# Where weight slots and activations lie in SBUF, in a two-block transformer kernel on one core

## The reference, cut to what matters

```python
def first_block(x, ...):                      # 272 tokens
    a = rmsnorm(h, norm1[i])
    proj = a @ w_in[i]                        # pooling, two kinds of attention
    h = h + jnp.concatenate([y_pool, y_fox, y_sb], axis=-1) @ w_out[i]
    a = rmsnorm(h, norm2[i])
    h = h + (jax.nn.silu(a @ w_gate[i]) * (a @ w_up[i])) @ w_down[i]
...
def second_block(x, ...):                     # 256 tokens
    h = swiglu(rmsnorm_2(x, norm_ffn1_pre[l]), w_ffn1_in[l], w_ffn1_out[l])
    x = x + FFN_RESIDUAL_SCALE * rmsnorm_2(h, norm_ffn1_post[l])
    h = mixer(rmsnorm_2(x, norm_mix_pre[l]), w_mix_in[l], ...)
    x = x + rmsnorm_2(h, norm_mix_post[l])
    h = swiglu(rmsnorm_2(x, norm_ffn2_pre[l]), w_ffn2_in[l], w_ffn2_out[l])
```

## Time and profile before

| | us |
|---|---|
| median of 3 runs | 800.4 |
| lowest, highest | 800.27, 800.4 |
| span of the profiled execution | 798.0 |

### The profile page before, as it was taken

How to read it: one execution, slowest core, us unless ns; L and a number is a source line. 1 busy time by engine, 2 the same in 40 slices (tenths; PEclk the granted TensorE clock), 3 DMA queues, 4 the chain that set the end, 5 groups by cost and what they waited for, 6 DMA issues and landing times.

```text
span 798.0 us, 12187 instructions
## 1 busy us (share of the span) xinstructions
PE 787.6 (99%) x4716; PEld 693.5 (87%) x4716; DVE 531.7 (67%) x621; ACT 429.6 (54%) x565; POOL 29.7 (4%) x35
## 2 busy tenths in 40 slices
PE   8999999999999999999999999999999999999997
PEld 8989989888888888888888887999988888888885
DVE  7865557766666567866666566766977766666665
ACT  6556658454544548753544536565557644454444
POOL 0000100000000000000000000002420000000000
PEclk9999999999999999999999999999999999999999
DMA  8633333655545543665545554452444655554521
GB/s 332 238 118 126 123 115 138 224 186 183 209 167 203 187 181 113 237 234 181 209 165 204 187 181 159 148 195 106 159 178 152 225 210 177 191 197 172 209 105 53
DMA packets 20798, 141.16 MB, mean 177 GB/s; under 512 B 2449, under 2 KB 2705, under 8 KB 4385
## 3 DMA queue, kind: packets, MB, share of 16 engines
q1 hardware_dynamic: 20192, 138.65, 48.3%
q0 software_dynamic: 576, 2.10, 0.8%
HBM read 139.69 MB, written 1.05 MB: 176 GB/s over the span
## 4 chain that ended last, share of the span: by engine, by line
PE 95%; DVE 2%; ACT 2%; issue 1%; DMA 1%; SPq 0%; DVEq 0%; ACTq 0%
PE ps L1457 93%; ACT whi L679 1%; PE ps L1463 1%; DMA raw<-wstream 1%; DVE x L1206 0%; ACT squared L694 0%; DVE xa L1018 0%; PE ps L1694 0%; DVE wlo L1007 0%; PE ps L1664 0%; PE ps L1896 0%; DVE xg L1201 0%; DVEq L270 0%; ACT L912 0%; PE ps L1696 0%
## 5 line engine op out<-in xcount | busy, mean ns | idle before, releaser
L1457 PE MATMUL ps<-xa,whi 128*128 128x512 f32 (+2 forms) x1744 | 488.8, 348 | 0.0
L1457 PE MATMUL ps<-xa,wlo 128*128 128x256 f32 (+1 forms) x1376 | 383.1, 282 | 0.0
L1007 DVE TENSOR_TENSOR wlo<-raw,whi 128x2048 fp32r<-128x2048 f32 x128 | 293.1, 2290 | 83.8 <-ACT whi L679 83.6
L1457 PEld LDWEIGHTS ps<-xa,whi 128*128 128x128 f32 x1744 | 302.5, 188 | 44.6 <-issue 2.1
L1457 PEld LDWEIGHTS ps<-xa,wlo 128*128 128x128 f32 x1376 | 258.7, 189 | 1.1
L679 ACT ACTIVATE whi<-raw 128x2048 fp32r<-128x2048 f32 x128 | 244.2, 1908 | 7.0 <-PE ps L1457 6.8
L1457 PE MATMUL ps<-whi,hhi 128*128 128x512 f32 x240 | 93.8, 391 | 0.0
L1457 PE MATMUL ps<-whi,hlo 128*128 128x512 f32 x240 | 93.7, 390 | 0.0
L1457 PE MATMUL ps<-wlo,hhi 128*128 128x512 f32 x240 | 93.5, 390 | 0.0
L873 ACT ACTIVATE hhi<-arena 128x512 fp32r<-128x512 f32 x30 | 19.0, 633 | 89.0 <-PE ps L1457 82.5
L859 ACT ACTIVATE arena<-ps 128x512 f32<-128x512 f32 x33 | 19.7, 596 | 87.5 <-PE ps L1457 87.3
(11 more groups left out here) (216 smaller groups left out, 531.3 us busy)
## 6 DMA issues: line engine op xcount, KB each, us to landing
raw<-wstream SPq DMA_DIRECT2D x128, 1024.0 KB, 4.8
gain_row<-rows_in POOLq DMA_DIRECT2D x4, 512.0 KB, 3.8
x<-x_in SPq DMA_DIRECT2D x2, 512.0 KB, 4.0
raw<-wstream SPq DMA_DIRECT2D x2, 512.0 KB, 5.5
out<-x SPq DMA_DIRECT2D x4, 256.0 KB, 2.1
xg<-const_in SPq DMA_DIRECT2D x1, 912.0 KB, 11.7
small<-small_in SPq DMA_DIRECT2D x1, 152.0 KB, 6.0
arena<-meta_in SPq DMA_DIRECT2D x1, 64.0 KB, 4.6
```

Source lines behind the costliest of these rows:

```text
L1007: nc.vector.tensor_tensor(wlo[slot][:], raw[slot][:], whi[slot][:].bitcast(F32), ALU.subtract).then_inc(lo_ready, 1)
L1457: return nc.tensor.matmul(o, lhsT, rhs, start=start, stop=stop, skip_group_check=True)
```

## The change

Three edits, all of them on addresses.

1. `hhi` and `hlo` are made ahead of the slots. The slots are made in pairs `whi0, wlo0, whi1, wlo1, whi2, wlo2`, with a gap of 40 numbers (160 bytes) ahead of `whi1` and ahead of `whi2`. What is made later lies 320 bytes further on than it would without the gaps.
2. `xn[k]`, for norm k, is a view into the same memory as `xa`, with blocks 512 columns (2048 bytes) apart instead of 544, that starts at column 92, 104, 0 or 120 of it (368, 416, 0 and 480 bytes). `norm` and `hi_of` write `xn[k]`.
3. All that reads the activations behind the first stage reads `xn[k]`: the gate and up tiles with k = 0, 1 and 3, the mixer's units with k = 2. The first block's projection keeps `xa` with its blocks 544 columns apart.

The instructions of each engine, their shapes, their order and their semaphores are the same as before.

```diff
+SLOT_GAPS = (0, 40, 40)
+XN_AT = (92, 104, 0, 120)
...
-        whi = [sb(f"whi{s}", [P, UNIT], F32R) for s in range(SLOTS)]
-        wlo = [sb(f"wlo{s}", [P, UNIT], F32R) for s in range(SLOTS)]
+        hhi = sb("hhi", [P, 2, 256], F32R)
+        hlo = sb("hlo", [P, 2, 256], F32R)
+        whi, wlo = [], []
+        for s, gap in enumerate(SLOT_GAPS):
+            if gap:
+                sb(f"gap{s}", [P, gap])
+            whi.append(sb(f"whi{s}", [P, UNIT], F32R))
+            wlo.append(sb(f"wlo{s}", [P, UNIT], F32R))
         xa = sb("xa", [P, KT, 2 * TOK], F32R)
         ya = sb("ya", [P, KT, 2 * SEQ], F32R)
-        hhi = sb("hhi", [P, 2, 256], F32R)
-        hlo = sb("hlo", [P, 2, 256], F32R)
...
+        xa_line = xa[:].rearrange("p k c -> p (k c)")
+        xn = [xa_line[:, c:c + KT * 2 * SEQ].rearrange("p (k c) -> p k c", k=KT) for c in XN_AT]
...
-                    nc.scalar.activation(xa[:, kt, 0:SEQ], turn_place(k, kt), ACT.Copy, scale=vec(gain, kt)).then_inc(xa_hi_ready, 1)
+                    nc.scalar.activation(xn[k][:, kt, 0:SEQ], turn_place(k, kt), ACT.Copy, scale=vec(gain, kt)).then_inc(xa_hi_ready, 1)
...
-                        xa[:, kt, SEQ:2 * SEQ], turn_place(k, kt), vec(gain, kt),
-                        xa[:, kt, 0:SEQ].bitcast(F32), ALU.mult, ALU.subtract).then_inc(xa_ready, 1)
+                        xn[k][:, kt, SEQ:2 * SEQ], turn_place(k, kt), vec(gain, kt),
+                        xn[k][:, kt, 0:SEQ].bitcast(F32), ALU.mult, ALU.subtract).then_inc(xa_ready, 1)
...
-            def paired_tile(bank, slot, a):
+            def paired_tile(bank, slot, a, k):
...
-                    mm(ps[:, bank, :], whi[slot][:, w], xa[:, kt, 0:2 * SEQ], kt == 0, False)
-                    ins = mm(ps[:, bank, 0:SEQ], wlo[slot][:, w], xa[:, kt, 0:SEQ], False, kt == KT - 1)
+                    mm(ps[:, bank, :], whi[slot][:, w], xn[k][:, kt, 0:2 * SEQ], kt == 0, False)
+                    ins = mm(ps[:, bank, 0:SEQ], wlo[slot][:, w], xn[k][:, kt, 0:SEQ], False, kt == KT - 1)
...
-                    mm(o, xa[:, kt, hi], whi[slot][:, w], kt == 0, False)
-                    mm(o, xa[:, kt, hi], wlo[slot][:, w], False, False)
-                    ins = mm(o, xa[:, kt, lo], whi[slot][:, w], False, kt == KT - 1)
+                    mm(o, xn[2][:, kt, hi], whi[slot][:, w], kt == 0, False)
+                    mm(o, xn[2][:, kt, hi], wlo[slot][:, w], False, False)
+                    ins = mm(o, xn[2][:, kt, lo], whi[slot][:, w], False, kt == KT - 1)
```

More of the change, by code:

```diff
@@ L1480, in spread_rstd, with columns_tile @@
                 ins.then_inc(rstd_spread, 1)
-            def columns_tile(o, slot, a, n, skip=0):
+            def columns_tile(o, slot, a, of, n, skip=0):
                 for kt in range(KT):
                     w = slice(kt * 256 + a * P, kt * 256 + (a + 1) * P)
-                    mm(o, whi[slot][:, w], xa[:, kt, skip:n], kt == 0, False)
-                    mm(o, whi[slot][:, w], xa[:, kt, n + skip:2 * n], False, False)
-                    ins = mm(o, wlo[slot][:, w], xa[:, kt, skip:n], False, kt == KT - 1)
+                    mm(o, whi[slot][:, w], of[:, kt, skip:n], kt == 0, False)
+                    mm(o, whi[slot][:, w], of[:, kt, n + skip:2 * n], False, False)
+                    ins = mm(o, wlo[slot][:, w], of[:, kt, skip:n], False, kt == KT - 1)
                 return ins
-            def paired_tile(bank, slot, a):
+            def paired_tile(bank, slot, a, k):
                 for kt in range(KT):
                     w = slice(kt * 256 + a * P, kt * 256 + (a + 1) * P)
-                    mm(ps[:, bank, :], whi[slot][:, w], xa[:, kt, 0:2 * SEQ], kt == 0, False)
-                    ins = mm(ps[:, bank, 0:SEQ], wlo[slot][:, w], xa[:, kt, 0:SEQ], False, kt == KT - 1)
+                    mm(ps[:, bank, :], whi[slot][:, w], xn[k][:, kt, 0:2 * SEQ], kt == 0, False)
+                    ins = mm(ps[:, bank, 0:SEQ], wlo[slot][:, w], xn[k][:, kt, 0:SEQ], False, kt == KT - 1)
                 return ins
@@ L1507, in first_paired_unit @@
                         w = slice(kt * 256 + a * P, kt * 256 + (a + 1) * P)
-                        mm(ps[:, bank + a, 0:SEQ], whi[slot][:, w], xa[:, kt, 0:SEQ], kt == 0, False)
-                        mm(ps[:, bank + a, 0:SEQ], wlo[slot][:, w], xa[:, kt, 0:SEQ], False, False)
+                        mm(ps[:, bank + a, 0:SEQ], whi[slot][:, w], xn[k][:, kt, 0:SEQ], kt == 0, False)
+                        mm(ps[:, bank + a, 0:SEQ], wlo[slot][:, w], xn[k][:, kt, 0:SEQ], False, False)
                 for kt in range(KT):
@@ L1513, in first_paired_unit @@
                         w = slice(kt * 256 + a * P, kt * 256 + (a + 1) * P)
-                        ins = mm(ps[:, bank + a, SEQ:2 * SEQ], whi[slot][:, w], xa[:, kt, SEQ:2 * SEQ], False, kt == KT - 1)
+                        ins = mm(ps[:, bank + a, SEQ:2 * SEQ], whi[slot][:, w], xn[k][:, kt, SEQ:2 * SEQ], False, kt == KT - 1)
                 return ins
@@ L1528, in first_columns_unit @@
                         w = slice(kt * 256 + c, kt * 256 + c + P)
-                        mm(o, whi[slot][:, w], xa[:, kt, 0:SEQ], kt == 0 and c == 0, False)
-                        mm(o, wlo[slot][:, w], xa[:, kt, 0:SEQ], False, False)
+                        mm(o, whi[slot][:, w], xn[k][:, kt, 0:SEQ], kt == 0 and c == 0, False)
+                        mm(o, wlo[slot][:, w], xn[k][:, kt, 0:SEQ], False, False)
                 for kt in range(KT):
@@ L1534, in first_columns_unit @@
                         w = slice(kt * 256 + c, kt * 256 + c + P)
-                        ins = mm(o, whi[slot][:, w], xa[:, kt, SEQ:2 * SEQ], False, kt == KT - 1)
+                        ins = mm(o, whi[slot][:, w], xn[k][:, kt, SEQ:2 * SEQ], False, kt == KT - 1)
                 return ins
@@ L1642, in _ @@
                         skip = META if query else 0
-                        columns_tile(ps[:, i % 2, skip:TOK], n % SLOTS, i % 2, TOK,
+                        columns_tile(ps[:, i % 2, skip:TOK], n % SLOTS, i % 2, xa, TOK,
                                      skip).then_inc(unit_used if i % 2 else even_full, 1)
@@ L1777, in ffn @@
                 base, unit0 = f * GROUPS, U_FFN[f]
+                norm = (0, 1, 3)[f]
                 def two_tiles(unit, slot, bank, spread=False):
                     pe.wait_ge(lo_ready, unit + 1)
-                    paired_tile(bank, slot, 0)
+                    paired_tile(bank, slot, 0, norm)
                     if spread:
-                        spread_rstd((0, 1, 3)[f], 2)
-                    paired_tile(bank + 1, slot, 1).then_inc(unit_used, 1)
+                        spread_rstd(norm, 2)
+                    paired_tile(bank + 1, slot, 1, norm).then_inc(unit_used, 1)
                 def gate(g, unit, slot, first):
@@ L1803, in ffn @@
                 pe.wait_ge(lo_ready, unit0 + 1)
-                first_paired_unit(4, unit0 % SLOTS, (0, 1, 3)[f]).then_inc(unit_used, 1)
+                first_paired_unit(4, unit0 % SLOTS, norm).then_inc(unit_used, 1)
                 up(0, unit0 + 1, (unit0 + 1) % SLOTS)
@@ L1846, in _ @@
                                 ins.then_inc(mgate_done, 1)
-                            ins = columns_tile(ps[:, bank, a * SEQ:(a + 1) * SEQ], n % SLOTS, a, SEQ)
+                            ins = columns_tile(ps[:, bank, a * SEQ:(a + 1) * SEQ], n % SLOTS, a, xn[2], SEQ)
                     ins.then_inc(unit_used, 1)
@@ L1853, in _ @@
                         for part in range(2):
-                            ins = mm(ps[0:BACK + 16, 2, 0:SEQ], gate_w[:, kt, :], xa[:, kt, part * SEQ:(part + 1) * SEQ],
+                            ins = mm(ps[0:BACK + 16, 2, 0:SEQ], gate_w[:, kt, :], xn[2][:, kt, part * SEQ:(part + 1) * SEQ],
                                      kt == 0 and part == 0, kt == KT - 1 and part == 1)
```

## The result

The changed kernel takes 804.32 us (median of 4 runs, 804.27 to 804.64), beside 800.34 us of the kernel before: ratio 1.0053, 95% interval 1.0042 to 1.0065. It is slower by 4.0 us. 795.5 was forecast, with a range up to 804.

A forecast was written before the change was run, and what follows sets the result against it. The prediction took TensorE's own matmul steps to bound the kernel, with nothing upstream late. Its terms, -4.5 - 1.1 + 0 + 0.7 = -4.9 us, gave 798.0 - 4.9 + 2.4 = 795.5 us, range 788 to 804.

The forecast's parts named there:

- What bounds the kernel: Whole kernel: the time is the sum of TensorE's own matmul steps, busy 787.6 of 798.0 us, with nothing upstream late.
- The case in which nothing moves: Rival for the whole kernel: the excess has no address cause, or gains and losses cancel; 800.4 us, chance 0.14.
- the rule quoted from the Trainium skill: TensorE has two independent read ports and never waits on anyone, so addresses don't matter and time stays at 800.4 us.
- (a): Gate and up units, three feed-forward networks: half of 1008 pairs gain 9 ns, -4.5 us; bounds -9.1 and +11.1.
- the case of the smooth rows: End of a down unit and next first pair: 0.2264 us per 512-column matmul, 0.340 a pair, taken as equal places.
- (b): Mixer's projections, 576 matmuls: one of three slot distances is the smooth case, -1.1 us; bounds -3.3 and +2.3.
- (c): First block's input projection, 480 matmuls: four places against three slots average out, 0; bounds -2.0 and +3.2 us.
- (d): Down and output units: networks one and two unchanged, third's down and ya matmuls get new distances; +0.7 us, at most +2.3.
- (e): VectorE and ScalarE writing the shifted slots: a tenth more on either stays hidden behind TensorE; nothing.
- A bad distance: Rival: up units (368, 416, 288) go to 0.360 us a pair, gate brings no gain; 806.6 us, chance 0.21.

The follow-up runs named there:

- e1_equal: Changed kernel without slot gaps and with every norm's activations at place 0 (byte address modulo 512, from weight slot 0): 805.87 us, ratio 1.0076.
- e5_wide: e1_equal with the low weight part moving 512 columns instead of 256 in every gate and up pair: 906.91 us in one run.
- e7_best: Changed kernel without slot gaps, activations of the three feed-forward networks at 288, of the mixer at 32: 797.89 us over 9 runs, ratio 0.9974.
- e6_order: e1_equal with the two tiles of a gate or up unit interleaved, so 512, 512, 256, 256 columns follow one another: 800.92 us in one run.
- s3_history: Changed kernel with slots 160 bytes from hhi and hlo, no gaps between slots, pairs at distances 0, 416 and 480: 806.15 us in one run.
- e4_shift: Changed kernel with 96 bytes put ahead of all operands of matmuls, distances between them unchanged: 804.26 us, ratio 1.0052.
- s2_fine: Changed kernel with SLOT_GAPS (0, 0, 2), XN_AT (2, 6, 0, 12); actual gate and up distances 40, 8; 56, 24; 48, 80: 804.41 us in one run.

## Why the prediction was wrong

*What bounds the kernel.* Right. TensorE's own steps make the time, nothing is waited for, and the addresses of its operands change those steps. The case in which nothing moves is out, and with it the rule quoted from the Trainium skill (SBUF — State Buffer, Who interferes with whom) as far as it would have TensorE's steps indifferent to addresses: with the same sequence of matmuls a pair took from 0.3465 to 0.3592 us as the mean of a unit, by the operands' places and by what they made of the units ahead. No run shows another engine holding TensorE up in these stages, so that part of the rule stands.

*(a), the term with the wrong sign.* It gave half of the pairs 9 ns, -4.5 us. Measured: 0.03 more for a gate or up unit on average, gate and up together 11.20 us in each network against 11.14, over all 1008 pairs +1.8 us. The step that failed is "the gate units come within 64 bytes of equal places, the case of the smooth rows". One pair in the earlier trace rows was smooth, and I took it for the case of equal places. It was the case of a pair behind a down unit; e1_equal has the same smooth pair at the head of a unit, and a mean of 0.3533 after it. The down rows, also smooth and at equal places, have no 256-column matmul, and e5_wide shows that at distance 0 this is what makes them smooth. They are the end of their unit besides: its first matmuls still vary, 0.228 to 0.236. I had noted the alternation of lengths, and dismissed it with that same first pair. The bulk of the trace, at distance 0 as at the other three, spoke against me: behind the first pair, every block at place 0 took 0.348 or 0.349 there.

*(b) and (c).* (b) promised -1.1 us; the mixer's columns didn't change in the mean, for the same reason. e7_best shows that the place could have given about what was hoped for. (c), 0, was right.

*(d), mis-sized.* +0.7 was put in and at most +2.3. Measured: 0.140 us for each of ten down units of the third network (5.613 against 5.473) +1.4, some +0.3 in the others, and 0.8 in the ya matmuls: +2.5. The bound was taken from the excess of the pairs, 4.5 ns a matmul; distance 160 costs a down matmul 6. And "nothing changes" for the first two networks was wrong: their down units kept their distance, but took over another rhythm from the up unit ahead (5.50 and 5.48 us, 5.47 before).

*(e)* was right: no wait on whi or wlo appears.

*Rivals.* "A bad distance" was the right side and nearly the right size (806.6 against 804.3), with a part of its mechanism: one unit of each network is at a bad distance. But it named the up units for all three, and it is the gate units in the second and third; and its price of 0.360 a pair was 0.353. That its size came close is partly luck. The last sentence of the prediction, that a law finer than the compared places would leave each unit a price of its own, is what happened, and it deserved a chance instead of a sentence: the terms (a) and (b) had rows for blocks at four places in turn, and the change used seven others (16, 368, 64, 416, 480, 288, 160).

The sum as measured: +1.8 in (a), about 0 in (b) and (c), +2.5 in (d), together +4.3 beside a span that grew by 4.6. What makes TensorE's steps follow these places stays open.

## What to carry to other kernels

Where one engine bounds the time and waits for nobody, compare the steps of equal instructions from start to start: here single pairs vary by up to 6% (0.340 to 0.361) for reasons that are in no wait and no busy share. A single smooth instance is not the steady state; look at which run of instructions it belongs to before a term is built on it. And a change of addresses can't be priced from other addresses: with rhythms that depend on 8 bytes and on the unit ahead, place the operands by trying a few places in each stage (here down units did best at distance 0, pairs at 16, 32, 288 or 416), and time the whole, since a unit changes the next one's rhythm. Expect fractions of a per cent: 0.26% here. Look at the granted clock of a single run before a difference of 1 us in it is read: e6_order hid 1.0 us there.

## What was not expected of the hardware

- Consecutive matmuls of 512 columns step by 0.2267 us when the stream is smooth, 6% over 512 / 2.4 GHz = 0.2133, at a granted clock of 1.00; in e5_wide all 32 steps of a gate unit do, as medians over the groups.
- In gate and up units at distances of all kinds, matmuls of 256 columns took 0.112 to 0.125 and those of 512 took 0.224 to 0.241, in cycles of one to four pairs that repeat to the nanosecond over a unit.
- In each of the settled cycles read here, the excess over 0.340 a pair comes in whole steps of 6.7 ns: one step a pair at distance 16 (0.3467), two at 368 (0.3533), three at 24 (0.3600), six over the three pairs of e1_equal (350, 361, 349 ns), five over four pairs in the kernel before (348, 351, 346, 348).
- Same addresses, same instructions, two rhythms, in strict turn from group to group (s3_history, first network: gate units of 5.56 and 5.64 us).
- A shift of both operands by 96 bytes changed no unit by more than 1 ns (e4_shift), where 8 bytes of distance went with 12 ns a pair (s2_fine).
